# Rotary partners of queries and keys by a matmul per slab in place of DMA copies

## The reference, cut to what matters

```
def partial_rope(x, cos, sin):
    half = C_ROT_DIMS // 2          # 8
    x1, x2, xp = x[..., :half], x[..., half:C_ROT_DIMS], x[..., C_ROT_DIMS:]
    return jnp.concatenate([x1 * cos - x2 * sin, x1 * sin + x2 * cos, xp], axis=-1)

    proj = h @ w_in[l]
    pa, pb, pc, pg = jnp.split(proj, GROUP_POINTS, axis=-1)
    ...
    q = partial_rope(qk_heads(q), cos, sin)
    k = partial_rope(qk_heads(k), cos, sin)
    ...
            z = jnp.einsum('bhqd,bhkd->bhqk', qb, kb).astype(f32) * scale
            return jax.nn.softmax(jnp.where(mask, z, -jnp.inf), axis=-1)
```

## Time and profile before

| | us |
|---|---|
| median of 3 runs | 1135.42 |
| lowest and highest | 1134.54, 1136.05 |
| the profiled execution | 1134.54 |
| its span | 1132.7 |

### The profile page before, as it was taken

The page is one execution under the profiler, slowest core; times in us unless marked ns, Lnnn a source line. Parts: engine busy times, 40 slices in busy tenths (PEclk is TensorE's granted clock), DMA queues, the critical chain, the costliest instruction groups (busy, mean ns, idle before and its releaser), DMA issues.

```text
span 1132.7 us, 26059 instructions
## 1 busy us (share of the span) xinstructions
PE 1088.8 (96%) x10078; PEld 1030.0 (91%) x10078; DVE 829.4 (73%) x1393; ACT 596.0 (53%) x883; POOL 10.5 (1%) x24
## 2 busy tenths in 40 slices
PE   8999999899999999999999999989999999999997
PEld 7888898699889999999999889978998999999996
DVE  6698485575768787788868975837666868778876
ACT  6851222646565665555687413145564656555555
POOL 0000000100000000000000000010000000000000
PEclk9999999999999999999999999998999999999998
DMA  7452322244435455655634413133453355565553
GB/s 279 135 165 76 112 76 94 66 149 138 143 129 187 140 197 185 186 184 169 190 128 142 157 58 110 61 85 109 136 166 131 131 186 168 186 187 183 169 186 112
DMA packets 46272, 164.00 MB, mean 145 GB/s; under 512 B 5904, under 2 KB 6080, under 8 KB 46192
## 3 DMA queue, kind: packets, MB, share of 16 engines
q1 hardware_dynamic: 44784, 160.88, 43.9%
q0 software_dynamic: 688, 0.81, 0.4%
q10 hardware_dynamic: 720, 1.14, 0.3%
HBM read 161.24 MB, written 1.05 MB: 143 GB/s over the span
## 4 chain that ended last, share of the span: by engine, by line
PE 73%; DVE 14%; ACT 7%; issue 5%; DMA 1%; ACTq 0%; DVEq 0%; SPq 0%
PE psum L457 73%; DVE sb_lo L1196 3%; ACT sb_rw L862 3%; ACT sb_inv L862 2%; ACT sb_hi L862 1%; DVE sb_rw L1274 1%; DVE sb_inv L1408 1%; DVE sb_yf L1422 1%; DVE sb_small L1477 1%; DMA sb_x<-x_t 1%; DVE sb_rw L1259 0%; ACT L862 0%; DVE sb_rw L1333 0%; DVE sb_inv L1400 0%; DVE sb_ol L1215 0%
## 5 line engine op out<-in xcount | busy, mean ns | idle before, releaser
L457 PE MATMUL psum<-sb_hh,sb_hi 128*128 128x256 f32 x1568 | 458.3, 292 | 11.1 <-DVE sb_rw L1259 4.2
L457 PE MATMUL psum<-sb_hl,sb_hi 128*128 128x256 f32 x1568 | 446.5, 285 | 0.0
L457 PE MATMUL psum<-sb_hh,sb_lo 128*128 128x256 f32 x1568 | 446.1, 285 | 0.0
L862 ACT ACTIVATE sb_hi<-sb_raw 128x1024 fp32r<-128x1024 f32 (+1 forms) x300 | 312.9, 1049 | 237.3 <-PE psum L457 233.1
L1196 DVE TENSOR_TENSOR sb_lo<-sb_raw,sb_hi 128x1024 fp32r<-128x1024 f32 x298 | 363.5, 1221 | 100.3 <-ACT sb_hi L862 98.4
L457 PEld LDWEIGHTS psum<-sb_hh,sb_hi 128*128 128x128 f32 x1568 | 303.4, 193 | 22.3 <-issue 16.3
L457 PEld LDWEIGHTS psum<-sb_hl,sb_hi 128*128 128x128 f32 x1568 | 303.7, 194 | 2.2 <-issue 2.2
L457 PEld LDWEIGHTS psum<-sb_hh,sb_lo 128*128 128x128 f32 x1568 | 303.6, 194 | 0.0
L457 PE MATMUL psum<-sb_oh,sb_hi 128*128 128x256 f32 x672 | 193.1, 287 | 7.9 <-DVE sb_ol L1525 4.7
L457 PE MATMUL psum<-sb_oh,sb_lo 128*128 128x256 f32 x672 | 190.8, 284 | 0.0
L457 PE MATMUL psum<-sb_ol,sb_hi 128*128 128x256 f32 x672 | 190.8, 284 | 0.0
(11 more groups left out here) (165 smaller groups left out, 1022.7 us busy)
## 6 DMA issues: line engine op xcount, KB each, us to landing
sb_raw<-w_stream SPq DMA_DIRECT2D x299, 512.0 KB, 3.8
sb_pm<-mix_par ACTq DMA_DIRECT2D x2, 512.5 KB, 3.5
y_t<-sb_rw SPq DMA_DIRECT2D x4, 256.0 KB, 2.3
sb_cf<-const_f SPq DMA_DIRECT2D x1, 739.0 KB, 9.3
sb_pm<-mix_par SPq DMA_DIRECT2D x1, 512.5 KB, 10.0
sb_raw<-w_stream SPq DMA_DIRECT2D x2, 256.0 KB, 4.0
sb_x<-x_t SPq DMA_DIRECT2D x2, 256.0 KB, 5.2
sb_x<-x_t SPq DMA_DIRECT2D x1, 512.0 KB, 6.7
```

What stands on the lines that cost most here:

```text
L457: return pe.matmul(out, lhsT, rhs, start=start, stop=stop, skip_group_check=True)
L862: return act.activation(out, in_, func, scale=scale, bias=bias, **kw)
```

## The change: what it does

The DMA copies, `PARTNER` and the two rope steps go. A constant 128x128 matrix `rope` (in place of a padding block of the constants) holds +1 and -1 so that its product with a slab's values gives each rotated dimension its partner with its sign. The emptying of a Cq or Ck slab now raises `rope_raw`. Behind the next dense slab, TensorE multiplies `rope` with the emptied slab, into the other half of that slab's own bank. In the next emptying, before its other work, VectorE waits for that (`rope_mm`), multiplies the values by the cosine and the product by the sine (128x256 each), adds them, and only then counts the bank as emptied. The last Ck slab is rotated in the step that empties Cv. The first score product waits for that count. The cosine and sine tables are as before but for the sign, which is in the matrix now.

```
-    pairs = [("rope", 0), ("bav", 0), ("btri", 1), ("rope", 1), ("bz", 2), ...
+    pairs = [("bav", 0), ("btri", 1), ("bz", 2), ...
...
-            for l in range(DEPTH):
-                pool.wait_ge(act_["o"], n_of("o", l, BT))
-                for i in range(2):
-                    pool.wait_ge(*n_out(l, (OUT_CQ, OUT_CK)[i]))
-                    for m in range(2):
-                        for b in range(2):
-                            to, of = HD * m + 8 * b, HD * m + 8 * (1 - b)
-                            pool.dma_start(PARTNER[i][to:to + 8], (qc, kc)[i][of:of + 8, :, :])\
-                                .then_inc(partner_in[i], 16)
+            with pool.Fori(0, DEPTH) as l:
...
+            def rope(l, n):
+                kind, c = DENSE[n]
+                pe.wait_ge(rope_raw, l * 2 * BT + (n - DENSE.index(("Cq", 0)) + 1))
+                mm(bank[BANK[OUT_OF[n][0]]][:, T:2 * T], cst("rope"), (qc if kind == "Cq" else kc)[:, c, :],
+                   True, True).then_inc(rope_mm, 1)
...
                 last.then_inc(slab_done, 1)
+                if n and DENSE[n - 1][0] in ("Cq", "Ck"):
+                    rope(l, n - 1)
...
                     if n == 0:
                         pe.wait_ge(*n_out(l, OUT_CV))
-                        pe.wait_ge(dve_["rope"], n_of("rope", l, 2))
+                        pe.wait_ge(*n_out(l, OUT_CK))
...
-            def rotate(l, i):
-                q = (qc, kc)[i]
-                dve.wait_ge(partner_in[i], 64 * l + 64)
-                own.mark(tt(PARTNER[i], PARTNER[i], rep(cst("sin"), BT), ALU.mult))
-                own.mark(tt(q[:, :, :], q[:, :, :], rep(cst("cos"), BT), ALU.mult))
-                own.wait()
-                tt(q[:, :, :], q[:, :, :], PARTNER[i], ALU.add).then_inc(dve_["rope"], 1)
+            def rotate(l, n):
+                kind, c = DENSE[n]
+                dst, i = (qc if kind == "Cq" else kc)[:, c, :], n - DENSE.index(("Cq", 0))
+                partner = bank[BANK[OUT_OF[n][0]]][:, T:2 * T]
+                dve.wait_ge(rope_mm, l * 2 * BT + i + 1)
+                own.mark(tt(dst, dst, cst("cos"), ALU.mult))
+                own.mark(tt(partner, partner, cst("sin"), ALU.mult))
+                own.wait()
+                tt(dst, dst, partner, ALU.add).then_inc(emptied["dve"], 1)
...
                 if n == A_SLABS:
                     mix_before(l, A_SLABS - 1)
+                if DENSE[n] == ("Cv", 3):
+                    rotate(l, DENSE.index(("Ck", 3)))
+                elif DENSE[n - 1][0] in ("Cq", "Ck"):
+                    rotate(l, n - 1)
...
                 elif kind in ("Cq", "Ck"):
                     tt((qc if kind == "Cq" else kc)[:, DENSE[n][1], :], b[:, 0:T], rs[:, 0:T], ALU.mult)\
-                        .then_inc(emptied["dve"], 1)
+                        .then_inc(rope_raw, 1)
...
+    for m in range(2):
+        for d in range(half):
+            rope[m * HD + d + half, m * HD + d] = -1.0
+            rope[m * HD + d, m * HD + d + half] = 1.0
```

More of the change, by code:

```diff
@@ L134, in mixing_steps @@
     steps += [("btri", 0), ("gn3",)] + dense(g0 + 2, g0 + 3) + [("bz", 1), ("gn4",)]
-    pairs = [("rope", 0), ("bav", 0), ("btri", 1), ("rope", 1), ("bz", 2), ("bav", 1), ("btri", 2), ("bz", 3), ("bav", 2), ("btri", 3), ("bav", 3)]
+    pairs = [("bav", 0), ("btri", 1), ("bz", 2), ("bav", 1), ("btri", 2), ("bz", 3), ("bav", 2), ("btri", 3), ("bav", 3)]
     steps += woven(pairs, list(range(g0 + 3, g0 + 2 * KT)))
@@ L188 @@
 X_STEPS = len(X_STEP)
-CF = {"ident": (0, 128), "ones": (128, 128), "bones": (256, 128), "pad0": (384, 128), "triN": (512, 128),
+CF = {"ident": (0, 128), "ones": (128, 128), "bones": (256, 128), "rope": (384, 128), "triN": (512, 128),
       "onesN": (640, 128), "cos": (768, 256), "sin": (1024, 256), "rowL": (1280, 128), "rowR": (1408, 64),
@@ L211 @@
 ACT_OWN = {"turn": 0, "layer": 20}
-DVE_OWN = {"turn": 8, "layer": 98}
+DVE_OWN = {"turn": 8, "layer": 110}
 class Own:
@@ L307, in hybrid_blocks @@
         SP = [inv[:, a:a + 768].rearrange("p (h n) -> p h n", h=2) for a in (768, 2304)]
-        PARTNER = [tiles(8), tiles(9)]
         PC = inv[:, 2304:3328].rearrange("p (s m n) -> p s m n", s=2, m=2)
@@ L356, in hybrid_blocks @@
         mixed = sem("mixed")
-        partner_in = [sem("query_partners_in"), sem("key_partners_in")]
+        rope_raw, rope_mm = sem("rope_raw"), sem("rope_mm")
         gates_ready = sem("gates_ready")
@@ L365, in hybrid_blocks @@
         pe_ = {k: sem("pe_" + k) for k in TIMES
-               if k not in ("D", "E", "xs", "gsig", "prepa", "prepb", "rk", "kkn", "kkq", "lora", "gn3", "gn4", "rope")}
+               if k not in ("D", "E", "xs", "gsig", "prepa", "prepb", "rk", "kkn", "kkq", "lora", "gn3", "gn4")}
         act_ = {k: sem("act_" + k) for k in TIMES if k not in ("D", "E", "xs", "norm")}
@@ L385, in hybrid_blocks @@
         OUT_BV, OUT_CV = OUT_OF[DENSE.index(("Bv", 3))][1], OUT_OF[DENSE.index(("Cv", 3))][1]
-        OUT_BK, OUT_CQ, OUT_CK, OUT_O = (OUT_OF[DENSE.index(k)][0] for k in (("Bk", 3), ("Cq", 3), ("Ck", 3), ("O", 0)))
+        OUT_BK, OUT_CK, OUT_O = (OUT_OF[DENSE.index(k)][0] for k in (("Bk", 3), ("Ck", 3), ("O", 0)))
         def ahead_in(split, l, i, n):
@@ L1491, in step @@
                     stt(a, b, small[:, f + 8:f + 9], a, ALU.mult, ALU.add).then_inc(dve_["cs"], 1)
-                elif kind == "rope":
-                    rotate(l, c)
                 elif kind == "crms":
@@ L1605, in constants @@
     put(cf, CF, "bones", row // HD == col // HD)
+    rope = np.zeros((P, P))
     half = HD // 8
+    for m in range(2):
+        for d in range(half):
+            rope[m * HD + d + half, m * HD + d] = -1.0
+            rope[m * HD + d, m * HD + d + half] = 1.0
+    put(cf, CF, "rope", rope)
     put(cf, CF, "triN", -(row >= col).astype(np.float32))
@@ L1614, in constants @@
             cos[m * HD + o:m * HD + o + half] = np.cos(ang)
-            sin[m * HD + o:m * HD + o + half] = np.sin(ang) if o else -np.sin(ang)
+            sin[m * HD + o:m * HD + o + half] = np.sin(ang)
     put(cf, CF, "cos", cos)
```

## The result

The changed kernel took a median of 1141.33 us (1140.07 to 1143.05, 5 runs) against 1135.42 us for the kernel before in the same comparison (1134.01 to 1136.05, 5 runs): ratio 1.0059, interval 1.0048 to 1.007. The profiled execution took 1142.97 us, its span is 1141.3.

The account below looks back on a forecast made before the run. TensorE was taken to bound the kernel, its matmuls filling 96% of the span. Per layer 1.95 + 3.12 + 0.77 + 0.65 + 1.34 + 0.65 = 8.48, for two layers +17.0 us: 1152.4 us, range 1144.0 to 1159.0.

Parts of the forecast that it names:

- What it removes: 16 small transfers and VectorE's old rotation instructions, 7.1 us per layer, claimed hidden behind TensorE: worth 0.
- nothing regained between 221 and 350: Sign of being right: the 8 to 9 us delay per layer persists through the G slabs and beyond.
- the rival of the clock: New stalls bring one or two more falls to 1.2 GHz per layer, 2.8 to 5.6 us on top, about 1156.6; chance 0.12.
- r, the price of an f32 matmul: TensorE's cost of each added 128x128 by 256 matmul between slabs: 0.65 us, bounds 0.45 to 0.75.
- The row of four at 0.45 each: The gate's low-rank product in the earlier trace, four such matmuls in 1.80 us, taken as the lower price.
- the 0.2 for standing alone: Surcharge on r because a single matmul has the switch into and out of the stream to itself.
- VectorE's terms: Three instructions of 256 columns before a slab's emptying: 1.14 us per rotation, bounds 1.0 to 1.4.
- 1.95 + 3.12 + 0.77: Delay up to the levels: three matmuls between slabs, three rotations where VectorE is packed, TensorE's wait at the first level.
- the stall ahead of D34: D34 waits for the rotation of Ck's third slab to free its bank: a new stall of 1.34 us.
- Hidden rotations: Rival: VectorE's rotations hide and only TensorE's 16 matmuls count, 10.4 us, 1145.8; chance 0.13.
- Faster by less work on VectorE: Rival: VectorE paces the G slabs, so 14.2 us come back against 10.4 for the matmuls, 1131.6; chance 0.02.
- No change: Rival: everything hides in TensorE's waits of the levels and the norm chain, 1135.4, within 0.2%; chance 0.03.

Follow-up runs that it names:

- e3: Kernel before without the rotation of queries and keys and its copies, the rope steps kept as empty places: 1132.48 us, ratio 0.9994.
- e6: Changed kernel with the old order of dense slabs (rope steps woven in, then dropped): 1148.63 us, ratio 1.0132.
- e5: The changed kernel, unchanged, run again beside the kernel before: 1141.76 us, ratio 1.0076.
- e4: Kernel before with its old rotation, but the dense slabs woven among nine steps as in the changed kernel: 1127.51 us, ratio 0.9946.
- e9: Old rotation with the changed kernel's order of slabs, repeated unchanged against the kernel before: 1127.30 us, ratio 0.9946.
- e10: Old rotation and new order plus one useless VectorE instruction, making the wait ahead of D41 2.09 us again, against the kernel before: 1132.18 us, ratio 0.9990.
- e7: Changed kernel without its 16 f32 matmuls, VectorE's three instructions per rotation kept, the second multiplying two constant tables: 1141.78 us, ratio 1.0067.
- e2: Kernel before plus eight unread f32 matmuls of the added form per layer, VectorE as before: 1143.18 us, ratio 1.01.
- e8: Kernel before with 14 useless matmuls in each of two TensorE waits per layer (ahead of gn2 and D41): 1131.72 us, ratio 0.9984.

## Why the prediction was wrong

**The step that failed** is "What it removes", and with it the larger part of the miss. It priced the work of the rope steps (transfers, VectorE) at 0, and e3 measured that as right. But what was removed was also two entries of a list over which the dense slabs are dealt out. That moved `bav0` in front of D41, and of what the prediction would have seen, "nothing regained between 221 and 350" is the sign that failed: 2.41 us came back there. The diff shows the edit of the list in its first line, and the earlier trace rows had the wait of 2.09 us and the slow records behind it; the prediction priced that fall of the clock at 1.4 us (the rival of the clock), but only as something that could be added. The order is worth 6.9 us in the changed kernel (e6 against e5) and 6.3 and 6.7 in the kernel before (e4, e9). In the traces each layer gives 0.8 us for the shorter wait and 1.5 for the fall behind D41 that is gone, 4.7 in all, and e10 gives back 4.9. Over the executions the clock is 0.0035 to 0.0056 higher, 2.7 to 4.3 us by the slope, so that between 0.7 and 2.6 us are not accounted for by the wait and the clock.

**r, the price of an f32 matmul**, was mis-sized: 0.43 us and not 0.65. D27 to D28 is 138.66 - 134.44 = 4.22 us, before 135.35 - 131.56 = 3.79. The row of four at 0.45 each was the right price. It already held the slower start of the next slab (the 0.19 in the sum), and the 0.2 for standing alone was a guess that no row showed. With five on the path per layer that is 2.2 us less in all.

**VectorE's terms were right.** The rotation is 1.14 us; the levels' last product is later by a share of 5.08 us, where 1.95 + 3.12 + 0.77 = 5.84 were forecast, or 5.18 with r = 0.43; the stall ahead of D34 moves it by 1.35 (forecast 1.34); behind it 0.48. The first layer's own cost is 7.34 us against 5 x 0.43 + 5 x 1.14 - 0.47 = 7.38. That the sum holds is also shown without the trace: e6 costs 15.3 us, twice 7.38 is 14.8. The Trainium skill (VectorE: DVE Perf Modes, the TRN2 errata) has a fixed cost for every VectorE instruction, and the trace agrees in direction: 256 columns take 0.33 to 0.34 us from start to start and 1024 take 1.18, not four times as much. Its table gave an estimated 1.05 us for a rotation, and the measured 1.14 decides.

**The account:** 17.0 forecast, less 2.2 (r), is 14.8, where e6 measured 15.3. Less 6.3 to 6.7 for the order, as e4 and e9 measured it in the kernel before, that is 8.1 to 8.5, and e5 shows +8.5. The comparison at the top had 5.9; its five executions of the kernel before have a median 1.6 us above the pooled one, and its five of the changed kernel are 0.8 below theirs.

**The rivals.** Hidden rotations: no, the stall and the levels show them on the path, and e7 has VectorE's part alone at +8.5 with a lower clock than e5's. The clock: it moved by several us, as this rival said, but upward, since the wait ahead of D41 got shorter. No fall stands behind the stalls of 0.49, 0.32, 0.65 and 1.16 us in the profiled execution, nor behind that of 1.16 in e5, e6 and e7. Where the stall ahead of the levels was longer, the rival isn't refuted: in e7, which has 1.54 us there, the first levels of the first layer run at a clock of 0.80 and lose 0.92 us. Faster by less work on VectorE: no (e3). No change: no.

**What stays open.** In which executions the clock falls at places other than D41: D33 ran at 0.61 in the kernel before and at 1.00 in the one after, but e4 and e9 are one kernel, and the window from 166 to 184, which holds D33, has 1.00 in e4 and 0.91 in e9. So D33's fall is not the change's. Nor is that behind the wait of 2.04 us always there: the first layer of e5, e7 and e2 has it, that of the changed kernel's own profile hasn't. Why the fillers of e8 gave only a part, other than that falls came elsewhere. What the steps further down the list add to the worth of the order. The stall ahead of D34 was not tested by itself; only the traces show it.

## What to carry to other kernels

A step that is dropped from a list over which other work is dealt out is also a change of order: write out the old and the new order around every wait of the bounding engine before pricing the diff. A small independent product put into a wait is worth its own time (here 0.8 us), and where the wait stands ahead of dense work it may be worth more by TensorE's clock (here 1.5 us); compare the mean granted clock of two kernels before explaining a few tenths of a per cent. And a price taken from a row of four of the same instruction needs no surcharge that no row shows.

## What the runs showed of the hardware

Two waits of TensorE per layer, one of 2.04 and one of 2.09 us, go with a mean clock of 0.990; with the second at 1.29 it is 0.995, and with that one lengthened to 2.09 again 0.991 (e4, e9, e10).

A fall costs 1.5 to 1.7 us in a stretch where TensorE bounds: 8.16 against 6.60 us for the same 36 records, 4.40 against 2.90 for a slab. The busy time of a window doesn't show it. From 166 to 184 us TensorE is busy for 17.27 us in the kernel before with a clock of 0.91 and for 17.27 in e4 with 1.00, but the first has got through 308 records and the second through 319, and from the last product of the levels to the `rhs` products behind D33 it takes 180.95 - 175.41 = 5.54 us in the one and 179.42 - 175.38 = 4.04 in the other.

```profile
166.00:184.00 18.00, 17.27 (x308) 16.26 (x305) 12.29 (x28) 1.06 (x1) 0.00 (x0) 0.91 0.10 31
```

```profile
166.00:184.00 18.00, 17.27 (x319) 16.14 (x315) 12.27 (x27) 1.33 (x2) 0.00 (x0) 1.00 0.14 40
```

Where TensorE waits for VectorE, a fall can cost nothing: the second group of 32 small products of the levels takes 1.64 us in e7 and 1.15 in the changed kernel, and the next group starts 3.27 us behind the first in the one and 3.26 in the other, the difference being idle time.

```profile
160.69 1.15 PE L448 MATMUL psum<-sb_inv 64*64 64x64 f32 x32 [1.54 <-DVE sb_inv L1403]
162.16 1.64 PE L448 MATMUL psum<-sb_inv 64*64 64x64 f32 x32 [0.32 <-DVE sb_inv L1411]
```

And adding work can cost more than the work: the 16 matmuls of e2 cost 9.4 us for 6.9 us of their own, with a clock 0.003 to 0.004 lower. The Trainium skill (TensorE: Matmul & The Clock Gate, Part 1) has the idle engine fall to half rate; the slow records behind the waits of e2 and e6 (0.21 us from start to start in place of 0.12) agree with it, and e10, whose profiled execution has 1.00 behind both waits of 2.09 us, shows that here such a wait doesn't bring a fall each time.
